# HGRN core of a two-block network on Trainium2: half products written in place, one buffer per level, and the decays computed beside the projection

## The chip, the cores and the metric

The kernel is written in Bass for one NeuronCore of a Trainium2 chip. The core has five engines with a queue of instructions each: TensorE (PE, with its weight loads shown apart as PEld), VectorE (DVE), ScalarE (ACT), GpSimd (POOL), and SyncE (SP), which here only issues DMAs. The engines meet at semaphores. The metric is the device time of one launch in microseconds (us).

## What is computed

Sequence length 512, model width 1024, batch 1. The change lies in the first layer (an "even" layer) of the first block: one projection of the input feeds an HGRN2 mixer with 4 heads of width 128 and a forgetting attention (FoX) with 8 heads of width 64; both are joined by an output projection. Three layers of other kinds follow and are not touched.

```python
proj = x @ ev_w_in[e]
qa, fa, ia, ga, qb, kb, vb, fb = split_cols(proj, [HALF] * 7 + [FOX_HEADS])
ya = hgrn2(qa, fa, ia, ga, lb_all[layer], ev_hgrn_norm_g[e])
yb = forgetting_attention(qb, kb, vb, fb, ev_fox_bf[e])
mix = jnp.concatenate([ya, yb], axis=-1) @ ev_w_out[e]

# hgrn2: the decays, and one step of its scan over chunks
log_f = jnp.log(lb + (1.0 - lb) * jax.nn.sigmoid(z))
k = (1.0 - lb) * jax.nn.sigmoid(-z)
b = jnp.cumsum(lt, axis=2)
o_inter = jnp.einsum('bhtk,bhkv->bhtv', qt * jnp.exp(b), state)
rel = b[:, :, :, None, :] - b[:, :, None, :, :]
decay = jnp.exp(jnp.where(causal, rel, -jnp.inf))
scores = jnp.einsum('bhtk,bhtsk,bhsk->bhts', qt, decay, kt)
o = o_inter + jnp.einsum('bhts,bhsv->bhtv', scores, vt)

# forgetting_attention: c is a running sum of log_sigmoid(f + b_f)
logits = logits + c[:, :, q0:q1, None] - c[:, :, None, :q1]
p = jax.nn.softmax(logits, axis=-1)
```

The decay between two positions differs by channel, so the kernel can't write the scores as one matmul. In chunks of 128 positions it splits the causal triangle into the diagonal (level 0) and 7 levels of off-diagonal blocks, whose side halves from one level to the next. In level i the decay of a pair is the product of a factor of the key (to the middle of its block) and one of the query (from there on), so each level is one set of matmuls of scaled keys with scaled queries, masked to the blocks of that level.

## The kernel before

`even_layer` (L1760) runs six stages one after the other, each closed by a barrier of all engines (`stage`, L64).

**Projection** (`linear_stage`, `linear_block`). 29 weight jobs of 512 KB are streamed. Per job ACT rounds the weights to a high part (L141), DVE subtracts to get the low part (L146), and PE does three matmuls for each of 8 tiles (L180 to L182). ACT writes the feature jobs 0 to 20 out of PSUM (L620), DVE the two groups of token jobs (L627). A `side` object can hang further work on each job j through `on_act`, `on_dve` and `on_pe`. The odd layer has one (`LruSide`), this layer has none.

**Constants** (`constants_stage`). DVE casts a few small masks.

**HGRN** (`hgrn_stage`, L1402). First a prologue: the lower bound `lb` from a softmax over three rows (L1522 to L1534), two sigmoids (L1448), the affine steps (L1537, L1540), one logarithm (L1468), and 16 scans of 128 columns for the running sums b (L1545). Then, per head, nine steps: for level i DVE subtracts the block's middle value from b (`take_diff`, L1557), ACT takes exp of the first half of each block with scale -1 (L1494) and of the second half with +1 (L1496), DVE multiplies all 512 columns with k (L1603) and POOL all 512 with q (L1636) into double buffers `ke` and `qe`. PE multiplies the two (L1679), DVE masks the result (`mask`, L1572), PE adds it into the output with v (`add_level`, L1652). `take_diff` runs one level ahead, and its two-deep buffers `diff` and `decay` are given back by L1603 and L1636. The ninth step is exp(b) for the state between chunks (L1477), followed by three state updates on DVE (L1616, L1619), POOL's `qd` (L1641) and three matmuls (L1708). Square (L1456), variance (L1661), logarithm and exp (L1461, L1464) and the gated write (`normed`, L1581, L1584) normalise the head before.

**FoX decay** (`fox_decay_stage`). One chain over DVE and ACT on 8 partitions, from L1721 to L1731, ends in `c_hi` and `c_lo`.

**Softmax attention** (`softmax_attention_stage`, L1284). 32 units, one for each block of 128 queries and head, with 128, 256, 384 and 512 keys for the blocks 0 to 3. Per unit PE writes q times k (L1786, contraction over 64 rows), adds c by two matmuls with a contraction over 8 rows each (L1789) and a bf16 mask (L1790), then transposes the exponentials of the unit before (L1322) and multiplies those of two units before with v (L1334). DVE finds the maximum (L1373), copies the transposed block (L1383), and scales the result (L1395); ACT does the exp (L1357).

**Output projection.** Another `linear_stage`. `keep_warm` (L346) is a helper that issues n matmuls of bf16 with 512 columns whose results nobody reads (L350); no stage from the first projection to the softmax calls it here.

## Time and profile before

| | |
|---|---|
| median of 3 runs | 3848.94 us (3837.36 to 3852.4) |
| profiled execution | 3850.37 us, of which its span in the trace is 3848.6 us |
| PE, DVE, ACT, POOL busy | 94%, 42%, 35%, 14% of the span |
| DMA | 76 GB/s over the span |

The busy shares are means over stages with different limits, so the rows further down are cut by stage. The table of stretches gives for each stretch its length, the busy time of each engine with the number of instructions, then `PEclk`, TensorE's granted clock as a share of 2.4 GHz (0.50 is the level of 1.2 GHz), the DMA share and GB/s. Timelines give start, duration, engine, line, operation, and in brackets the idle time before it and what ended it.

### The profile page before, as it was taken

What the parts mean: (1) busy time and instruction counts of PE and PEld (TensorE: products, weight loads), DVE (VectorE), ACT (ScalarE), POOL (GpSimd) and SP (SyncE); (2) the same over time, 40 slices, a digit from 0 to 9 for tenths busy, and PEclk for the clock granted to TensorE, in tenths of its full rate; (3) what the DMA queues carried; (4) which work ended last, traced back from release to release, by engine and by line L of the source; (5) the groups of instructions that cost most, each with busy time, mean ns of one, the idle gap of its engine ahead of it and who ended that gap; (6) DMA issues with size and microseconds to landing.
All of it is one profiled execution on the core that took longest, in us unless ns stands there. A gap on an engine that the chain in (4) does not pass through costs nothing. (4 is left out here: it accounts for less than half of the span.)

```text
span 3848.6 us, 42102 instructions
## 1 busy us (share of the span) xinstructions
PE 3598.5 (94%) x15648; PEld 2825.8 (73%) x15662; DVE 1619.7 (42%) x2091; ACT 1334.2 (35%) x1864; POOL 552.4 (14%) x446
## 2 busy tenths in 40 slices
PE   8878999998889999899998889999999999789998
PEld 7675668886666888688885468887788875578885
DVE  2284443335554333433345743335333235743335
ACT  3232232224553222433232543324333233533324
POOL 0030121101022110221000012202221000022202
PEclk9985899999999999999999899999999999899999
DMA  4200123322112332233220023322233220123322
GB/s 136 81 1 1 44 71 98 107 85 67 49 44 77 98 107 79 77 94 108 82 91 34 13 83 96 106 97 75 90 96 108 84 79 28 33 82 94 109 81 72
DMA packets 77745, 294.18 MB, mean 76 GB/s; under 512 B 8624, under 2 KB 11184, under 8 KB 77360
## 3 DMA queue, kind: packets, MB, share of 16 engines
q1 hardware_dynamic: 77616, 292.45, 23.9%
q8 instruction: 82, 1.34, 0.1%
q14 instruction: 47, 0.39, 0.0%
HBM read 290.32 MB, written 2.10 MB: 76 GB/s over the span
## 5 line engine op out<-in xcount | busy, mean ns | idle before, releaser
L146 DVE TENSOR_TENSOR w_low<-w_raw,w_high 128x1024 fp32r<-128x1024 f32 (+4 forms) x513 | 672.7, 1311 | 1578.5 <-ACT w_high L141 1578.5
L180 PE MATMUL bank<-x_high,w_high 128*128 128x512 f32 x2856 | 1130.4, 396 | 74.5 <-POOL x_low L224 22.0
L181 PE MATMUL bank<-x_low,w_high 128*128 128x512 f32 x2856 | 1120.4, 392 | 0.0
L182 PE MATMUL bank<-x_high,w_low 128*128 128x512 f32 x2856 | 1120.3, 392 | 0.0
L141 ACT CAST w_high<-w_raw 128x1024 fp32r<-128x1024 f32 (+4 forms) x513 | 555.0, 1082 | 872.8 <-PE bank L182 867.1
L180 PEld LDWEIGHTS bank<-x_high,w_high 128*128 128x128 f32 x2856 | 541.0, 189 | 206.4 <-issue 38.2
L182 PEld LDWEIGHTS bank<-x_high,w_low 128*128 128x128 f32 x2856 | 541.1, 189 | 113.3
L181 PEld LDWEIGHTS bank<-x_low,w_high 128*128 128x128 f32 x2856 | 541.9, 190 | 112.0 <-issue 2.1
L182 PE MATMUL bank<-hidden_high,w_low 128*128 128x512 f32 x1056 | 411.4, 390 | 0.0
L180 PE MATMUL bank<-hidden_high,w_high 128*128 128x512 f32 x1056 | 411.4, 390 | 0.0
L181 PE MATMUL bank<-hidden_low,w_high 128*128 128x512 f32 x1056 | 411.4, 390 | 0.0
L182 PEld LDWEIGHTS bank<-hidden_high,w_low 128*128 128x128 f32 x1056 | 198.3, 188 | 41.1
L180 PEld LDWEIGHTS bank<-hidden_high,w_high 128*128 128x128 f32 x1056 | 198.3, 188 | 41.1
L181 PEld LDWEIGHTS bank<-hidden_low,w_high 128*128 128x128 f32 x1056 | 198.3, 188 | 40.9
L901 POOL TENSOR_TENSOR hidden_and_gated<-hidden_and_gated,rstd 128x512 f32<-128x512 f32 x88 | 113.6, 1290 | 413.0 <-ACT hidden_and_gated L879 413.0
L905 POOL TENSOR_TENSOR hidden_low<-hidden_and_gated,hidden_high 128x512 f32 (+1 forms) x88 | 113.2, 1286 | 376.1 <-ACT hidden_high L883 376.1
L741 POOL TENSOR_TENSOR hidden_low<-hidden_and_gated,hidden_high 128x512 f32 (+1 forms) x44 | 56.9, 1294 | 434.9 <-ACT hidden_high L713 434.9
L883 ACT CAST hidden_high<-hidden_and_gated 128x512 f32 (+1 forms) x88 | 54.7, 622 | 175.5 <-DVE hidden_and_gated L939 175.5
L879 ACT ACTIVATE hidden_and_gated<-hidden_and_gated 128x512 f32<-128x512 f32 x88 | 55.6, 632 | 160.7 <-DVE hidden_and_gated L934 160.6
L713 ACT CAST hidden_high<-hidden_and_gated 128x512 f32 (+1 forms) x44 | 27.3, 621 | 212.3 <-DVE hidden_and_gated L767 212.3
L1357 ACT ACTIVATE probs<-bank,exp_bias 128x512 f32<-128x512 f32 (+3 forms) x64 | 38.8, 607 | 172.9 <-DVE exp_bias L1376 172.9
L1373 DVE TENSOR_REDUCE top<-bank 128x1 f32<-128x512 f32 (+3 forms) x64 | 37.9, 592 | 111.8 <-PE bank L1790 60.2
(481 smaller groups left out, 3799.9 us busy)
## 6 DMA issues: line engine op xcount, KB each, us to landing
w_raw<-in_stream SPq DMA_DIRECT2D x381, 512.0 KB, 3.5
w_raw<-in_stream SPq DMA_DIRECT2D x96, 704.0 KB, 4.0
w_raw<-in_stream SPq DMA_DIRECT2D x16, 384.0 KB, 3.1
dft_positions<-in_dft SPq DMA_DIRECT2D x2, 2048.0 KB, 7.4
w_raw<-in_stream SPq DMA_DIRECT2D x4, 576.0 KB, 3.7
h<-in_x SPq DMA_DIRECT2D x8, 256.0 KB, 6.0
w_raw<-in_stream SPq DMA_DIRECT2D x16, 128.0 KB, 2.1
out<-result SPq DMA_DIRECT2D x4, 512.0 KB, 2.6
```

What stands on the lines that cost most here:

```text
L141: self.nc.scalar.copy(self.hi[:, j % 2, 0:size], self.raw[:, s, 0:size]).then_inc(S.high_ready, 1)
L146: self.nc.vector.tensor_tensor(self.lo[:, j % 2, 0:size], self.raw[:, j % RAW_SLOTS, 0:size], self.hi[:, j % 2, 0:size].bitcast(F32), ALU. ...
L180: nc.tensor.matmul(out, lhs[0], rhs[0], start=start, stop=False)
L181: nc.tensor.matmul(out, lhs[0], rhs[1], start=False, stop=False)
L182: return nc.tensor.matmul(out, lhs[1], rhs[0], start=False, stop=stop)
L741: nc.gpsimd.tensor_tensor(hlo[:, at, :], hidden[:, u % 2:u % 2 + 1, :], hhi[:, at, :].bitcast(F32), ALU.subtract).then_inc(S.hid_low, 1)
L879: nc.scalar.activation(gated[:, u // 2, :], gated[:, u // 2, :], ACT.Silu).then_inc(S.gate_ready, 1)
L883: nc.scalar.copy(hhi[:, bass.ds(u // 2 + 2 * k, 1), :], hidden[:, u // 2, :]).then_inc(S.hid_high, 1)
L901: nc.gpsimd.tensor_tensor(gated[:, u % 2, :], gated[:, u % 2, :], C.rstd[:, :], ALU.mult).then_inc(S.gate_scaled, 1)
L905: nc.gpsimd.tensor_tensor(hlo[:, at, :], hidden[:, u % 2:u % 2 + 1, :], hhi[:, at, :].bitcast(F32), ALU.subtract).then_inc(S.hid_low, 1)
L1357: nc.scalar.activation(probs[:, n % 2, 0:keys(n)], C.bank[n % 2][:, 0:keys(n)], ACT.Exp, bias=bias[:, n:n + 1], scale=scale, accum_out=tot ...
L1373: nc.vector.tensor_reduce(top[:, n:n + 1], C.bank[n % 2][:, 0:keys(n)], AX.X, ALU.max).then_inc(S.top_ready, 1)
```

## The change

1. `DecaySide` is a side object of the projection. It takes over the whole HGRN prologue, the constants and the FoX decay: on ACT the first sigmoid (all four heads at once) after job 7, the second after job 12, the logarithm after job 14, FoX's steps after jobs 22, 23 and 25; on DVE the matching steps, four scans each after jobs 16 to 19. The level masks are fetched at the projection's start. The stages `constants_stage` and `fox_decay_stage` are gone.
2. After the last projection matmul PE issues 14 warm matmuls (`end_pe`); in the HGRN stage 8 stand ahead of the last variance and 24 behind it.
3. Level i has a buffer X[i] of its own. `take_diff` writes it, ACT's exps, DVE's product with k (first halves only, 256 columns) and POOL's with q (second halves only) are done in it in place, and PE reads it as both operands. `take_diff` runs two levels ahead, across heads. `normed(h)` moves to two heads later.
4. On PE a level's product now stands ahead of the `add_level` of two levels before, and the end of a head no longer stands in one piece: its last additions and its state product come behind the first levels of the next head.
5. In FoX `c_hi` and `c_lo` lie in one tile (partitions 0 to 7 and 64 to 71, zeros between), so one matmul over 72 rows takes the place of two over 8. It comes first, the mask second, q times k last.

```diff
+            if side:
+                side.end_pe(nc, C, pe, S)
...
-        diff, decay = C.ring[:, 0:2, :], C.ring[:, 2:4, :]
-        qe = sb("q_decayed", [P, 2, T])
-        ke = sb("k_decayed", [P, 2, T])
+        NL = LEVELS + 1
+        N = HALF_T * NL
+        more = sb("level_inputs", [P, NL - 4, T])
+        X = [C.ring[:, i, :] if i < 4 else more[:, i - 4, :] for i in range(NL)]
...
+                def decayed_k(m):
+                    h, i = m // NL, m % NL
+                    dve.wait_ge(S.decay_ready, 2 * (m + 1))
+                    x, kx = (halves(X[i], i)[0], halves(k[h], i)[0]) if i else (X[0], k[h])
+                    nc.vector.tensor_tensor(x, kx, x, ALU.mult).then_inc(S.k_ready, 1)
...
+                take_diff(0)
+                take_diff(1)
+                for m in range(N):
+                    h, i = m // NL, m % NL
+                    if m + 2 < N:
+                        take_diff(m + 2)
+                    decayed_k(m)
+                    if m >= 2:
+                        mask(m - 2)
+                    if i == 6:
+                        states(h)
+                    if h >= 2 and i == 1:
+                        normed(h - 2)
...
+                    if i:
+                        pool.wait_ge(S.decay_ready, 2 * (m + 1))
+                        x, qx = halves(X[i], i)[1], halves(q[h], i)[1]
+                        nc.gpsimd.tensor_tensor(x, qx, x, ALU.mult).then_inc(S.q_ready, 1)
...
+                add_level(N - 2)
+                add_level(N - 1)
+                keep_warm(nc, C, C.bank[0], 8)
                 variance(HALF_T - 1)
+                keep_warm(nc, C, C.bank[0], 24)
...
+    NEGATED, PLUS, LOGS, SCAN, FOX = 7, 12, 14, 16, 21
...
+        if j == self.NEGATED:
+            act.wait_ge(S.evacuated, 4 + 8)
+            nc.scalar.activation(self.kk[:, :, :], prj[:, 4:8, :], ACT.Sigmoid,
+                                 scale=-1.0).then_inc(S.negated, 1)
...
-                nc.tensor.matmul(bank[:, 0:keys], prj[r, 12 + t, qb * P:(qb + 1) * P],
-                                 prj[r, 16 + t, 0:keys], start=True, stop=False)
-                for part in (c_hi, c_lo):
-                    nc.tensor.matmul(bank[:, 0:keys], C.pick(h), part[:, 0:keys], start=False, stop=False)
+            nc.tensor.matmul(bank[:, 0:keys], C.pick_fox(h), c_parts[:, 0:keys], start=True, stop=False)
+            nc.tensor.matmul(bank[:, qb * P:keys], C.ident_bf, C.mask_after, start=False, stop=False)
+            return nc.tensor.matmul(bank[:, 0:keys], prj[r, 12 + t, qb * P:(qb + 1) * P],
+                                    prj[r, 16 + t, 0:keys], start=False, stop=True)
```

On ACT, in the projection, around jobs 7 and 8, the queue before reads (L141 is the high part of a weight job, L620 the write of a feature job):

```order
L620 ACTIVATE projections<-bank 128x512
L141 CAST w_high<-w_raw 128x1024
L620 ACT_TABLE_LOAD
L620 ACTIVATE projections<-bank 128x512
L141 CAST w_high<-w_raw 128x1024
```

and after the change (L622 is the same write, L1681 the first sigmoid):

```order
L622 ACTIVATE projections<-bank 128x512
L1681 ACT_TABLE_LOAD
L1681 ACTIVATE hgrn_k<-projections 128x2048
L141 CAST w_high<-w_raw 128x1024
L622 ACT_TABLE_LOAD
L622 ACTIVATE projections<-bank 128x512
```

A table load and a sigmoid of 2048 columns moved in between a job's write and the next job's high part; the same pattern stands after jobs 12 and 14.

On DVE, at the end of a head and the start of the next in the HGRN core, before (L1557 difference, L1603 product with k, L1572 mask, L1616 and L1619 state, L1596 level 0's product with k):

```order
L1603 TENSOR_TENSOR k_decayed<-hgrn_k,hidden_and_gated 128x512
L1572 TENSOR_TENSOR masked<-bank,level_masks 128x512 x2
L1616 COPY state<-bank 128x128
L1619 SCALAR_TENSOR_TENSOR state<-state,sq_sum_and_last,bank 128x128 x2
L1557 TENSOR_TENSOR hidden_and_gated<-projections 128x512 x2
L1596 TENSOR_TENSOR k_to_end<-hgrn_k,hidden_and_gated 128x512
L1572 TENSOR_TENSOR masked<-bank,consts 128x512
```

and after (L1498 difference, L1507 product with k, L1513 mask, L1527 and L1530 state):

```order
L1507 TENSOR_TENSOR level_inputs<-hgrn_k,level_inputs 128x128x2
L1513 TENSOR_TENSOR masked<-bank,level_masks 128x512
L1527 COPY state<-bank 128x128
L1530 SCALAR_TENSOR_TENSOR state<-state,sq_sum_and_last,bank 128x128 x2
L1498 TENSOR_TENSOR hidden_and_gated<-projections 128x512
L1507 TENSOR_TENSOR level_inputs<-hgrn_k,level_inputs 128x256
L1513 TENSOR_TENSOR masked<-bank,level_masks 128x512
L1498 TENSOR_TENSOR hidden_and_gated<-projections 128x512
L1507 TENSOR_TENSOR hidden_and_gated<-hgrn_k,hidden_and_gated 128x512
L1513 TENSOR_TENSOR masked<-bank,level_masks 128x512
```

The state updates now stand between levels 6 and 7 with the next head's difference already taken, and the products of levels 1 to 7 have 256 columns (as 128x128x2, 128x256).

On PE, where the HGRN stage ends, before (L1652 adds a level, L1708 the state product, L1661 the variance):

```order
L1652 MATMUL bank<-masked,hgrn_v 128x128 x8
L1708 MATMUL bank<-sq_sum_and_last,state 128x128 x3
L1661 MATMUL bank<-rstd,consts 128x512
L1435 UNCONDITIONAL_BRANCH
```

and after (L1584, L1594, L1601 are the same three, L350 the warm matmuls, then FoX's c, mask and q times k):

```order
L1584 MATMUL bank<-masked,hgrn_v 128x128 x12
L1594 MATMUL bank<-sq_sum_and_last,state 128x128 x3
L350 MATMUL bank<-consts_bf 128x512 x8
L1601 MATMUL bank<-rstd,consts 128x512
L350 MATMUL bank<-consts_bf 128x512 x24
L1440 UNCONDITIONAL_BRANCH
L1310 UNCONDITIONAL_BRANCH
L1798 MATMUL bank<-fox_c_parts,ident_fox 128x128
L1799 MATMUL bank<-consts_bf 128x128
L1800 MATMUL bank<-projections 128x128
```

32 warm matmuls stand around the last variance, and the softmax follows them with no stage between.

## Rows read from the trace of the kernel before

**Rows 1.** Table of stretches, by stage, columns as told above.

```profile
178.50:200.80 22.30, 2.09 (x9) 1.78 (x8) 13.88 (x43) 9.79 (x7) 0.00 (x0) 0.58 0.06 21
200.80:300.50 99.70, 80.32 (x570) 74.79 (x570) 88.94 (x114) 40.75 (x84) 42.25 (x32) 0.87 0.00 1
...
316.80:435.10 118.30, 116.80 (x416) 75.68 (x416) 45.52 (x160) 23.02 (x69) 0.00 (x0) 0.59 0.00 1
```

**Rows 2.** Timeline of ACT and DVE in the projection, one of the jobs.

```profile
43.79 0.60 ACT L620 ACTIVATE projections<-bank 128x512 f32<-128x512 f32 x1 [3.91 <-PE bank L182]
44.29 1.04 ACT L141 CAST w_high<-w_raw 128x1024 fp32r<-128x1024 f32 x1
...
45.36 1.23 DVE L146 TENSOR_TENSOR w_low<-w_raw,w_high 128x1024 fp32r<-128x1024 f32 x1 [4.21 <-ACT w_high L141]
```

**Rows 3.** Timeline, from the projection's end to the first level.

```profile
178.54 2.48 DVE L627 COPY fox_v<-bank 128x512 f32<-128x512 f32 x4 [3.08 <-PE bank L182]
181.93 0.36 DVE L1752 CAST consts_bf<-masks 128x384 bf16<-128x384 f32 x1 [0.90 <-PEq L64]
...
185.04 1.28 ACT L1448 ACT_TABLE_LOAD   x1
...
186.33 1.91 ACT L1448 ACTIVATE hgrn_k<-projections 128x2048 f32<-128x2048 f32 x1
```

**Rows 4.** Timeline of one level of the HGRN core (DVE, ACT, POOL).

```profile
262.58 0.68 DVE L1572 TENSOR_TENSOR masked<-bank,level_masks 128x512 f32<-128x512 f32 x1
...
263.19 1.52 DVE L1557 TENSOR_TENSOR hidden_and_gated<-projections 128x512 f32<-128x512 f32 x1
264.63 0.68 DVE L1603 TENSOR_TENSOR k_decayed<-hgrn_k,hidden_and_gated 128x512 f32<-128x512 f32 x1
...
265.60 1.27 POOL L1636 TENSOR_TENSOR q_decayed<-projections,hidden_and_gated 128x512 f32<-128x512 f32 x1 [1.44 <-ACT hidden_and_gated L1496]
265.83 1.58 DVE L1557 TENSOR_TENSOR hidden_and_gated<-projections 128x512 f32<-128x512 f32 x1
```

**Rows 5.** Stretches at the core's start and where its first head ends.

```profile
206.00:212.00 6.00, 5.34 (x25) 5.35 (x26) 5.29 (x6) 2.53 (x7) 2.77 (x2) 0.50 0.01 3
...
225.00:230.00 5.00, 2.88 (x23) 2.48 (x22) 4.86 (x8) 2.28 (x6) 1.47 (x2) 0.97 0.01 3
```

**Rows 6.** Timeline of DVE and PE at the end of the HGRN stage.

```profile
298.55 0.73 DVE L1619 SCALAR_TENSOR_TENSOR state<-state,sq_sum_and_last,bank 128x128 f32<-128x128 f32 x2
...
301.42 2.07 PE L1661 MATMUL bank<-rstd,consts 128*128 128x512 f32 x2 [0.88 <-ACT rstd L1456]
...
306.97 0.69 DVE L1584 TENSOR_TENSOR projections<-projections 128x512 f32<-128x512 f32 x1
```

**Rows 7.** Timeline: warm matmuls elsewhere in the kernel.

```profile
491.93 4.91 PE L350 MATMUL bank<-consts_bf 128*128 128x512 bf16 x22 [1.90 <-PEq L64]
```

**Rows 8.** Stretches of the softmax: blocks 0 to 3, its hot part, its tail.

```profile
316.80:333.30 16.50, 16.48 (x60) 12.09 (x60) 6.78 (x33) 4.52 (x16) 0.00 (x0) 0.50 0.01 1
333.30:360.00 26.70, 26.70 (x89) 17.81 (x88) 10.33 (x42) 5.37 (x19) 0.00 (x0) 0.50 0.00 0
360.00:397.00 37.00, 37.00 (x113) 22.99 (x112) 12.25 (x40) 5.87 (x18) 0.00 (x0) 0.50 0.00 1
397.00:411.50 14.50, 14.50 (x38) 7.59 (x38) 4.12 (x12) 1.55 (x4) 0.00 (x0) 0.50 0.01 1
415.00:427.10 12.10, 12.10 (x67) 7.57 (x66) 6.63 (x18) 3.12 (x8) 0.00 (x0) 1.00 0.00 0
427.10:435.10 8.00, 6.53 (x42) 4.71 (x41) 3.84 (x13) 1.80 (x5) 0.00 (x0) 1.00 0.00 0
```

**Rows 9.** Timeline of PE in one unit with 512 keys, at the full clock.

```profile
423.90 1.12 PE L1786 MATMUL bank<-projections 64*128 64x512 f32 x2
424.95 0.49 PE L1789 MATMUL bank<-fox_c_high,ident_parts 8*128 8x512 f32 x1
425.29 0.39 PE L1789 MATMUL bank<-fox_c_low,ident_parts 8*128 8x512 f32 x1
```

476 lines of the change are left out of this document (227 added, 249 removed).

## The prediction

> **What bounds the kernel now.** The busy shares of the page say little here (PE 94% of the span), since all that changes lies in the first 435 us; what follows is the same program. So I read the table of stretches first, cut by stage, then timelines of single steps. Four things are to be seen.
>
> The projection is PE's: a job takes 5.44 us, in which ACT works 1.6 us and DVE 1.23 us [rows 2]. Side work fits there nearly free.
>
> From 178.5 to 200.8 us PE is busy 2.1 us of 22.3 [rows 1]: two stage ends of about 0.9 us, the constants, and the prologue, a chain over ACT and DVE [rows 3]. The FoX decay is another such chain, from DVE's last write at 307.66 to 316.8 us [rows 6, 1].
>
> The HGRN core, 200.8 to 300.5, is DVE's: 88.9 of 99.7 us busy [rows 1]. A level takes 2.70 us from the end of one difference (263.19 + 1.52 = 264.71) to the end of the next (267.41) [rows 4]. That isn't three operations of 0.68. The difference of 1.58 us lies over POOL's product, which ends at 266.87, and it ends 0.54 us after it; alone it would take 0.68 like the mask. So the level is 0.89 (difference to POOL's start, through ACT's two exps) + 1.27 (POOL) + 0.54. At a head's end comes a hole in which PE is busy 2.88 of 5 us and its clock falls [rows 5].
>
> The softmax, 118.3 us, is PE's: busy nearly all of it, at 0.50, that is 1.2 GHz, for its first 95 us, and at 1.00 for its last 20 [rows 8]. Eight units with 384 keys take 37.0 us at the low level, 4.6 each; one with 512 keys takes only 3.20 at the high one (423.90 to 427.10, where the last begins) [rows 8, 9].
>
> **The change, part by part.** The sum is made against the profiled execution (span 3848.6, run 3850.4, which is 1.4 above the median of 3848.9; the saving is then taken off the median).
>
> Side work in the projection. After jobs 7, 12 and 14 ACT has, between a job's write and the next high part, one table load of 1.28 and one function over 2048 columns of 1.91 us [rows 3]. Chain per job: write 0.50 to the next start, 3.19 for the side work, high part 1.06, low part 1.23 = 5.98 against 5.44 [rows 2]. PE waits 0.54 us each, 1.6 in all. All other side work (DVE's products, 4 scans a job, small FoX steps with one table load each) fits DVE's 4.2 or ACT's 3.9 us of idle time per job. Bounds: 0 if slack in the two weight slots hides it, 6 if DVE's side steps add their wait each time. The level masks' DMA moves ahead of the weights' but lands long before its use.
>
> Here a row and the Trainium skill can be weighed: the load's row says 1.28 us [rows 3]. The page ScalarE: Activation LUTs gives two figures, about 2.7 us in its section Terms and 1283 ns in What ACT_TABLE_LOAD costs. By the first, each of the three steps would be 1.4 us longer and PE's wait 5.8 us instead of 1.6; the trace agrees with the second.
>
> Prologue. PE ends at 178.5 + 1.6 = 180.1; 14 warm matmuls at 4.91/22 = 0.22 us [rows 7] and their wait end at 183.3, 0.7 after DVE's last copy (182.6); one stage end of 0.95 [rows 3], so the first difference starts at 184.3 instead of 200.8. Gain 16.5.
>
> Core. POOL's product has 256 columns: between 0.64 (half of 1.27) and 1.27; DVE's 512 columns take 0.68 and 128-column updates 0.37 [rows 6], so a fixed part exists; I take 0.74. DVE's product with k drops from 0.6 to 0.34 effective. DVE's own step is then 0.6 + 0.34 + 0.6 = 1.55, and a difference is ready to start 0.94 after the last one, just after POOL has started (0.89). So the level is 0.89 + 0.74 + 0.54 = 2.17, with 1.55 (POOL never in the way) and 2.70 (half products cost as much as whole ones) as ends. Sum: start to the first k product 2.65 (difference, table load, exp); 32 levels x 2.17 = 69.4; states 4 x 1.05 = 4.2; POOL's whole `qd` in the way 4 x 0.6 = 2.4; two `normed`, each two operations like the one of 0.69 [rows 6], = 2.9; ACT's normalisation at two head changes x 2 = 4 (logarithm, exp and two table loads are some 4 us: 4.17 from the variance to DVE's end, less 1.4 of DVE, plus a load; with the wait for the variance that is longer than two levels of lead); PE's cold start 3 (before, it ran at 0.50 for its first 6 us too; 26 weight loads took 5.35 us there and 22 took 2.48 later [rows 5], so the 16 of a level 3.3 instead of 1.8); last masks, additions and state product 2.5. Total 91, against 99.7: gain 8.7, with 71 to 110 as ends. So the core gains least; the holes between heads go, but DVE remains late next, with PE close (1.8 us of weight loads per level at the full clock).
>
> A rule speaks against this part: the page GPSIMD Engine Reference of the Trainium skill, section 7, says of kernels written for POOL's own cores that reads of SBUF with a step over 8 bytes cost half as much again per element. If the second halves' runs of 2 to 8 columns fell under it, 12 of 28 products would be 0.37 us longer and the core 4 us. No run here shows POOL on such runs yet.
>
> Tail. 8 warm matmuls 1.7, variance 1.0 at the full clock (2.07 at half [rows 6]), 24 warm matmuls 5.3, which end after the normalisation's ACT and DVE steps (4.2 us behind the variance). 8.2 against 7.1 (300.54 to 307.66): loss 1.1.
>
> FoX decay. 9.1 us become one stage end of 0.9: gain 8.2.
>
> Softmax. This decides. Fewer matmuls: one of two c matmuls goes, 0.34 us at the full clock with 512 keys [rows 9]. At half it lies between 0.34 and 0.68; I take 0.57, and 0.3, 0.36 and 0.45 with 128, 256 and 384 keys. If the clock stays as it was, that is 8 x (0.3 + 0.36 + 0.45) + 3 x 0.57 + 5 x 0.33 = 12. But PE now comes in at the full clock: warm matmuls until 0.9 us before the first score. Then a unit is, for blocks 3 to 0: 3.20 - 0.33 = 2.9 (PE); about 2.2 (PE); 1.7 and 1.45 (DVE: maximum, copy, scale and two small steps, no longer under PE). 7 x 2.9 + 8 x (2.2 + 1.7 + 1.45) + tail 7.7 = 71 against 118.3: gain 47.5.
>
> Sum: 16.5 + 8.7 - 1.1 + 8.2 + 47.5 = 79.8. Profiled 3850.4 - 79.8 = 3770.6; off the median 3769.
>
> **The rivals.** (A) *The clock stays up through the softmax*: 3769. For it: where the clock fell in this trace, PE had been busy about half of 5 us or less [rows 5]; once up in block 3 it stayed, and with 128 keys PE would have work for over half of each 1.45 us. Against: 95 us of nearly full busy time didn't bring it up before [rows 8], so contractions over 8 or 64 rows and short matmuls may count for little, and block 0 may lose it.
>
> (B) *It falls in block 0 and returns in block 1 or 2*, as the denser units allow: blocks 0 and 1 near the old pace less c (14 + 24), the rest half and half: 91 instead of 71, so 3789.
>
> (C) *It falls and returns only in block 3*, as before: softmax 106, so 3849 - 45 = 3804.
>
> (D) *The half products don't shorten a level* (POOL's time is not by columns, or its lock hits the k product too): 32 x 0.53 = 17 more on A, 3786.
>
> (E) *Slower than before*: PE's clock stays at 1.2 GHz from the start of the core to the output projection. Place: levels. PE then needs 3.3 us a level where DVE needs 2.17, which is 36, and 10 for variance, transposes and state at half; warm matmuls +10; softmax without its hot end 116, +45: 3769 + 101 = 3870. It decides once cold time costs over 80 us. Against it: the same level stream brought the clock up within 7 us after every fall [rows 5].
>
> (F) *The change doesn't do what it says*: side work isn't hidden because DVE's and ACT's side steps wait on each other and hold the next weight job. 29 jobs; each microsecond of wait per job is one lost. It would take over 2.7 us on every job to lose all; I see it on 3 jobs. A bad case is +10: 3779, inside A's range.
>
> **How the numbers follow.** A 0.55, B 0.12, C 0.17, D (with the clock up) 0.11, E 0.02, other 0.03. I forecast A: 3769. A alone spans 3753 (level near 1.8, no wait in the projection, softmax 67) to 3782. The range must reach over B, D and C to leave out no more than 2 in 10: 3753 to 3807. A measurement of this kernel tells 0.5% (19 us) from no change; faster than 3829.7 are A to D and F: 0.95; within 0.5% only C with a bad core: 0.03; slower, E: 0.02.
>
> **What would show each step right or wrong.** Projection: PE's end at 180 us, three waits for w_low of about 0.5 us, table loads of 1.28. Prologue: first difference near 184 us. Core: half products of 0.34 to 0.42 on DVE and 0.64 to 0.8 on POOL, a step near 2.2 us, `PEclk` 1.00 from some 10 us after the start without dips at heads, length near 91. Softmax: `PEclk` 1.00 from its first unit and a length near 71; 106 with 0.50 in blocks 0 to 2 would be C. Everything after the softmax: the same 3413 us. I would be most wrong if the clock in block 0 doesn't hold, or if the level isn't set by the pair of DVE and POOL.

## The result, and the profile after

The changed kernel took **3782.59 us** (median of 4 runs, 3781.46 to 3785.99) against 3850.67 us for the kernel before (4 runs, 3837.36 to 3857.32). The ratio is 0.9829, with a 95% interval of 0.9802 to 0.9856: 68 us faster, where 80 had been forecast. The profiled execution took 3781.46 us, with a span of 3779.6.

First the table of stretches of the changed kernel, which answers to [rows 1 and 8]. The columns are as there: the stretch, its length, busy time of PE, PE's weight loads, DVE, ACT and POOL with their instructions, the granted clock, DMA share and GB/s. The lines are the prologue, the core, the softmax, and the part of the softmax at the low clock.

```profile
181.60:185.60 4.00, 2.97 (x14) 1.18 (x13) 2.49 (x4) 0.00 (x0) 0.00 (x0) 1.00 0.00 0
185.60:265.30 79.70, 72.55 (x578) 68.26 (x580) 70.14 (x114) 40.29 (x84) 34.74 (x32) 0.96 0.01 1
274.40:360.50 86.10, 84.46 (x384) 58.99 (x384) 46.09 (x160) 21.74 (x68) 0.00 (x0) 0.74 0.00 1
277.60:321.60 44.00, 44.00 (x151) 31.23 (x151) 20.66 (x83) 9.75 (x35) 0.00 (x0) 0.50 0.00 1
360.50:3779.60 3419.10, 3245.75 (x13956) 2544.64 (x13970) 1420.44 (x1727) 1205.18 (x1634) 502.98 (x406) 0.97 0.25 80
```

Set against the trace of before this is where the 69.0 us of the span went. The stages follow each other without a gap, so the differences add up. The table compares one execution of each kernel; the four runs of the kernel before lie 20 us apart, those of the changed kernel 4.5.

| stretch | before | after | gained | forecast |
|---|---|---|---|---|
| start to the last evacuation's start | 178.5 | 181.6 | -3.1 | -1.6 |
| to the first difference (prologue) | 22.3 | 4.0 | 18.3 | 18.1 |
| core | 99.7 | 79.7 | 20.0 | 8.7 |
| core's end to the first score | 16.3 | 9.1 | 7.2 | 7.1 |
| softmax | 118.3 | 86.2 | 32.1 | 47.5 |
| the rest, the same program | 3413.5 | 3419.1 | -5.6 | 0 |

(The forecast's 16.5 for the prologue already holds the 1.6 that the projection loses, and its last tail terms, -1.1 and 8.2, stand together here.)

**The core.** The timeline of DVE through two levels, which answers to [rows 4] (start, length, engine, line, operation):

```profile
205.35 0.68 DVE L1513 TENSOR_TENSOR masked<-bank,level_masks 128x512 f32<-128x512 f32 x1
205.95 0.68 DVE L1498 TENSOR_TENSOR hidden_and_gated<-projections 128x512 f32<-128x512 f32 x1
206.55 0.41 DVE L1507 TENSOR_TENSOR hidden_and_gated<-hgrn_k,hidden_and_gated 128x256 f32<-128x256 f32 x1
206.88 0.68 DVE L1513 TENSOR_TENSOR masked<-bank,level_masks 128x512 f32<-128x512 f32 x1
207.49 0.68 DVE L1498 TENSOR_TENSOR level_inputs<-projections 128x512 f32<-128x512 f32 x1
208.09 0.95 DVE L1507 TENSOR_TENSOR hidden_and_gated<-hgrn_k,hidden_and_gated 128x256 f32<-128x256 f32 x1
208.96 0.68 DVE L1513 TENSOR_TENSOR masked<-bank,consts 128x512 f32<-128x512 f32 x1
```

and POOL's in the same stretch:

```profile
205.13 0.89 POOL L1569 TENSOR_TENSOR hidden_and_gated<-projections,hidden_and_gated 128x256 f32<-128x256 f32 x1 [0.25 <-ACT hidden_and_gated L1467]
207.46 1.29 POOL L1569 TENSOR_TENSOR hidden_and_gated<-projections,hidden_and_gated 128x256 f32<-128x256 f32 x1 [1.45 <-ACT hidden_and_gated L1467]
209.00 0.73 POOL L1569 TENSOR_TENSOR level_inputs<-projections,level_inputs 128x256 f32<-128x256 f32 x1 [0.24 <-ACT level_inputs L1467]
```

Before, the difference was what POOL held up, 1.58 us instead of 0.68. Now it takes 0.68 here. Over the whole core a difference takes 0.73 us in the mean, where it took 1.13. The two engines still get in each other's way, but on short work: where POOL's product starts together with a difference, the product takes 1.29 instead of 0.73, and DVE's product behind it 0.95 instead of 0.41 (0.75 in the mean of all 28). From mask to mask a level took 1.53 (205.35 to 206.88) and 2.08 us (206.88 to 208.96). What is left is one wait at two of the three changes of heads, 3.00 and 2.50 us; the longer one:

```profile
220.13 0.68 DVE L1498 TENSOR_TENSOR hidden_and_gated<-projections 128x512 f32<-128x512 f32 x1
223.81 0.69 DVE L1507 TENSOR_TENSOR hidden_and_gated<-hgrn_k,hidden_and_gated 128x512 f32<-128x512 f32 x1 [3.00 <-ACT hidden_and_gated L1463]
```

ACT is late there because it stands before its logarithm until PE's variance comes (the first line ends with 4.43 us of idle time), loads the table of the exponential, and only then turns to the next head:

```profile
220.63 0.69 ACT L1453 ACTIVATE rstd<-bank,eps 128x512 f32<-128x512 f32 x1 [4.43 <-PE bank L1601]
221.34 1.28 ACT L1456 ACT_TABLE_LOAD   x1
222.63 0.63 ACT L1456 ACTIVATE rstd<-rstd 128x512 f32<-128x512 f32 x1
223.17 0.61 ACT L1463 ACTIVATE hidden_and_gated<-hidden_and_gated 128x512 f32<-128x512 f32 x1
```

**From the core to the softmax.** PE's timeline, which answers to [rows 6]. The last five lines are the start of the fourth unit of block 0; up to 277.35 the same three score matmuls took 0.30, 0.23 and 0.49 us.

```profile
265.35 1.67 PE L350 MATMUL bank<-consts_bf 128*128 128x512 bf16 x7
266.86 1.02 PE L1601 MATMUL bank<-rstd,consts 128*128 128x512 f32 x2
267.72 5.34 PE L350 MATMUL bank<-consts_bf 128*128 128x512 bf16 x24
274.37 0.30 PE L1798 MATMUL bank<-fox_c_parts,ident_fox 72*128 72x128 f32 x1 [1.30 <-PEq L64]
274.51 0.23 PE L1799 MATMUL bank<-consts_bf 128*128 128x128 bf16 x1
274.67 0.49 PE L1800 MATMUL bank<-projections 64*128 64x128 f32 x2
...
277.35 0.46 PE L1798 MATMUL bank<-fox_c_parts,ident_fox 72*128 72x128 f32 x1
277.61 0.33 PE L1799 MATMUL bank<-consts_bf 128*128 128x128 bf16 x1
277.87 0.79 PE L1800 MATMUL bank<-projections 64*128 64x128 f32 x2
278.60 0.47 PE L1324 MATMUL bank<-consts,probs 128*128 128x128 f32 x1
278.86 0.63 PE L1336 MATMUL bank<-fox_v,probs_t 128*128 128x128 f32 x2
```

PE comes in at 2.4 GHz, as forecast, with a pause of 1.30 us, and 3 us later it is at 1.2 GHz. It stays there for 44 us, into block 2. That is rival B of the prediction, not its forecast A.

**The rest.** Same program, 5.6 us longer. Read in stretches of 2 us, its time at the low clock grew from 188.7 to 211.7 us; in the stick-breaking stage, for one, the kernel before had three spells with 17.1 us together (1014 to 1040 us in), and the changed kernel has nine with 37.6 us (939 to 1039 us in).

### The profile page after: what moved, and what is told of

It is laid out like the page before. It is cut to its first block and busy times, and to the rows that moved or that the text cites. A ratio compares the mean times of both kernels' runs of the same rounds, so it can differ in the third digit from the quotient of the medians.

```text
span 3779.6 us, 41993 instructions
## 1 busy us (share of the span) xinstructions
PE 3575.7 (95%) x15660; PEld 2809.0 (74%) x15676; DVE 1601.5 (42%) x2095; ACT 1334.5 (35%) x1864; POOL 544.8 (14%) x446
## 5 line engine op out<-in xcount | busy, mean ns | idle before, releaser
L141 ACT CAST w_high<-w_raw 128x1024 fp32r<-128x1024 f32 (+4 forms) x513 | 555.0, 1082 | 867.9 <-PE bank L182 862.7
L769 DVE TENSOR_TENSOR hidden_and_gated<-bank,hidden_and_gated 128x512 f32<-128x512 f32 x44 | 30.4, 692 | 120.6 <-PE bank L182 120.6
```

The lines of the kernel that those rows point to most:

```text
L141: self.nc.scalar.copy(self.hi[:, j % 2, 0:size], self.raw[:, s, 0:size]).then_inc(S.high_ready, 1)
L769: nc.vector.tensor_tensor(hidden[:, u // 2, :], C.bank[u][:, :], gated[:, u // 2, :], ALU.mult).then_inc(S.hid_ready, 1)
```

## The experiments

All were single profiled runs beside the kernel before, but for the last two, which were timed five and six times. The table gives the lengths of the stages, read as above; "cold" is the time at 1.2 GHz from the core's end to the softmax's end, read in stretches of 2 us, and the stretch in which it lies.

| kernel | run | prologue | core | to first score | softmax | cold | rest |
|---|---|---|---|---|---|---|---|
| changed kernel | 3781.5 | 4.0 | 79.7 | 9.1 | 86.2 | 44 (276-322) | 3419.1 |
| a1 no end warm | 3781.8 | 4.0 | 79.7 | 7.4 | 87.7 | 51 (270-324) | 3419.2 |
| a2 two c matmuls | 3810.1 | 4.0 | 80.5 | 9.1 | 116.5 | 92 (278-372) | 3415.6 |
| a3 warm beside units | 3757.0 | 4.0 | 79.7 | 9.1 | 70.8 | 3 (276-282) | 3410.2 |
| a4 128 rows | 3778.4 | 4.0 | 79.8 | 9.1 | 86.1 | 44 (278-324) | 3415.5 |
| c1 before, half products | 3845.6 | 24.6 | 86.3 | 15.4 | 124.0 | 119 (296-416) | 3413.8 |
| c2 one level ahead | 3783.8 | 4.0 | 78.0 | 9.1 | 92.4 | 58 (276-336) | 3415.6 |
| c3 decays apart | 3800.7 | 28.8 | 79.4 | 8.6 | 86.2 | 44 (298-344) | 3416.4 |
| c4 q.k first | 3781.8 | 4.0 | 79.7 | 9.1 | 89.5 | 48 (276-326) | 3415.8 |
| d1 split and root later | 3758.4 | 4.0 | 74.6 | 9.1 | 75.3 | 21 (266-290) | 3415.6 |
| d2 four warm units | 3756.7 | 4.0 | 80.7 | 9.1 | 67.6 | 0 | 3410.4 |
| d3 all three | 3763.0 | 4.0 | 74.7 | 7.4 | 81.2 | 31 (262-294) | 3413.6 |
| e1 end warm kept | 3761.9 | 4.0 | 74.7 | 9.1 | 77.7 | 24 (268-292) | 3415.3 |

### The clock in the softmax

The theory after the result: the clock is lost at the change of stages or in block 0's thin matmuls, and where it returns depends on how many matmuls a unit has. The rivals: the 32 warm matmuls at the core's end cost more than they bring; the number of rows over which the c matmul runs counts.

**a1**: without the warm matmuls at the core's end.

```
-                keep_warm(nc, C, C.bank[0], 8)
                 variance(HALF_T - 1)
-                keep_warm(nc, C, C.bank[0], 24)
```

> The changed kernel without the 8 and 24 warm matmuls at the end of the HGRN stage. In the changed kernel the softmax began at the full clock and lost it 3.3 us later. If the warm matmuls buy only those 3 us, the softmax is 1 to 4 us longer (87 to 90 instead of 86.2) and the HGRN tail 3 to 4 us shorter (9.1 to about 6), so the first 360 us end within 2 us of the changed kernel. If they also bring forward the return of the clock in block 2, the softmax is over 8 us longer.

Measured: the way to the first score is 1.7 us shorter, not 3 to 4, the softmax 1.5 us longer, and the run as long as the changed kernel's. The clock fell 6 us earlier, ahead of the softmax, and came back at nearly the same place. In this kernel the 32 matmuls are neither gain nor loss: the clock is low for most of block 0 with them and without.

**a2**: the decay's parts by two matmuls over 8 rows, as in the kernel before.

```
-            nc.tensor.matmul(bank[:, 0:keys], C.pick_fox(h), c_parts[:, 0:keys], start=True, stop=False)
...
+            for part in (c_parts[0:8, :], C.c_lo[:, :]):
+                nc.tensor.matmul(bank[:, 0:keys], C.ident_parts[0:8, h:h + 1].to_broadcast([8, P]), part[:, 0:keys],
+                                 start=False, stop=False)
```

> The changed kernel with FoX's scores as before: q times k first, then c_hi and c_lo as two matmuls over 8 rows each, then the mask. Theory 1 (what counts for the clock's return is how much of the array's height and time is filled; two thin matmuls dilute it): the clock returns only in block 3, as before (some 14 us into it), and the softmax takes 100 to 108 us instead of 86.2. Theory 2 (the return depends on what came before the softmax, not on the c matmul): it returns in block 2 and the softmax takes 86.2 + 12 for the additional matmuls at most 98.

Measured: 30 us longer in the softmax. That is far more than the matmuls themselves, some 12 us by the prediction's sum. The clock now stays low until block 3, 92 us instead of 44. All three kernels with two c matmuls (this one, the kernel before, and c1 below) got it back only there.

**a3**: two warm matmuls (bf16, 384 columns) beside each unit of block 0, one beside each of block 1, written into the bank of the turned probabilities ahead of them.

```
+                        for w in range(warm[units[m][0]]):
+                            nc.tensor.matmul(C.bank[2 + m % 2][:, 0:3 * P], C.ident_bf, C.con_bf[:, 0:3, :],
+                                             start=True, stop=True)
                         pe.wait_ge(S.exp_done, m + 1)
...
+        softmax_attention_stage(nc, C, HEADS, HD, scores, vb, prj, 4, True, 1.0, warm=(2, 1, 0, 0))
```

> The changed kernel with warm matmuls of 384 columns inside the softmax, in TensorE's wait for the exp: two in each unit of block 0, one in each of block 1. If the thin work of block 0 is what loses the clock, it stays at 1.00 through the softmax, which then takes 70 to 77 us instead of 86.2 and the program is 10 to 16 us shorter than the changed kernel. If the clock falls anyway (the gap at the stage's start is what loses it), the softmax is longer than 86 by the warm matmuls at the low clock, 88 to 95.

Measured, stretches of 2 us over the start of this kernel's softmax, then its whole softmax:

```profile
276.00:278.00 2.00, 2.00 (x13) 1.52 (x11) 1.23 (x6) 0.97 (x6) 0.00 (x0) 0.80 0.00 0
278.00:280.00 2.00, 2.00 (x9) 1.40 (x9) 0.91 (x5) 0.31 (x3) 0.00 (x0) 0.50 0.00 0
280.00:282.00 2.00, 2.00 (x14) 1.66 (x13) 1.31 (x7) 0.43 (x3) 0.00 (x0) 0.84 0.00 0
282.00:284.00 2.00, 2.00 (x15) 1.51 (x14) 1.65 (x9) 0.67 (x4) 0.00 (x0) 1.00 0.00 0
...
274.30:345.20 70.90, 69.40 (x408) 48.80 (x408) 45.94 (x160) 21.78 (x68) 0.00 (x0) 0.98 0.00 1
```

The clock falls at the same moment as in the changed kernel and is back after 3.4 us of low clock in all. Neither of the two cases expected is what happened: it neither stayed up nor stayed down. The softmax takes 70.8 us, close to the prediction's 71 for case A, a state that the changed kernel doesn't reach; but these 70.8 hold the low spell and 24 warm matmuls.

**a4**: the c matmul over 128 rows instead of 72, the further ones zero.

```
-        c_parts = ctx.enter_context(sbuf(nc, "fox_c_parts", [72, T], F32R))
+        c_parts = ctx.enter_context(sbuf(nc, "fox_c_parts", [P, T], F32R))
...
-        C.pick_fox = lambda h: C.ident_fox[:, h:h + 1].to_broadcast([72, P])
+        C.pick_fox = lambda h: C.ident_fox[:, h:h + 1].to_broadcast([P, P])
```

> The changed kernel with the c tile padded to 128 rows of which the added ones are zero, so the c matmul runs over 128 rows instead of 72, with the same columns. Theory 1a (rows of the array, even with zeros in them, count for the clock): the clock returns earlier, in block 1, and the softmax takes 70 to 80 us. Theory 1b (only columns streamed per time count): it returns at the same place within 4 us and the softmax stays at 85 to 88.

Measured: no difference (86.1 against 86.2 us, 44 us at the low clock in both). Rows of zeros changed neither the softmax's time nor the clock.

**c4**: one c matmul, but q times k ahead of it, as in a2. It asks whether a2's late return came from the order.

```
-            nc.tensor.matmul(bank[:, 0:keys], C.pick_fox(h), c_parts[:, 0:keys], start=True, stop=False)
-            nc.tensor.matmul(bank[:, qb * P:keys], C.ident_bf, C.mask_after, start=False, stop=False)
-            return nc.tensor.matmul(bank[:, 0:keys], prj[r, 12 + t, qb * P:(qb + 1) * P],
...
+            nc.tensor.matmul(bank[:, 0:keys], prj[r, 12 + t, qb * P:(qb + 1) * P],
+                             prj[r, 16 + t, 0:keys], start=True, stop=False)
+            nc.tensor.matmul(bank[:, 0:keys], C.pick_fox(h), c_parts[:, 0:keys], start=False, stop=False)
+            return nc.tensor.matmul(bank[:, qb * P:keys], C.ident_bf, C.mask_after, start=False, stop=True)
```

> The changed kernel with the three matmuls of a score in another order: q times k first, then the one matmul over the 72 rows of parts of the decay, the mask last. Two causes are to be told apart for the clock's earlier return in the softmax (44 us cold in the changed kernel, 92 us with two matmuls for the decay's parts and q times k first). By the number of matmuls: the clock returns in block 2 at about 320 us, and the softmax takes 84 to 90 us. By the order: it returns only in block 3, and the softmax takes 105 to 117 us.

Measured: the clock returned in block 2 and the softmax took 89.5 us. So the order isn't it; the second matmul over 8 rows is what goes with the late return. How firm that is, the end of this section says: five kernels with one and the same softmax program lie between 21 and 58 us at the low clock.

### The core and the prologue

**c1**: the kernel before, with the half products alone. The cut shows k's; q's on POOL is made the same way with the other halves, and both operands are cleared once ahead of the loop.

```
-                            nc.vector.tensor_tensor(ke[:, i % 2, :], k[h], decay[:, m % 2, :],
+                            nc.vector.tensor_tensor(half_of(ke[:, i % 2, :], i, 0), half_of(k[h], i, 0),
+                                                    half_of(decay[:, m % 2, :], i, 0),
...
```

> The kernel before with one part of the change alone: k's and q's products of a level over the half of the columns that the next level's matmul needs (256 of 512), their two operands each cleared once ahead of the loop. The differences still run one level ahead through the small buffers, the extra two steps per head and the decays stay where they were. Theory 1 (the products were the core's bound: per level the difference 0.89 us, the k product 0.73, the mask 0.54 on VectorE, and a q product of half the length on GpSimd that no longer bars VectorE): the core falls from 99.7 us to about 84 to 88, that is three quarters or more of the 20 us that the core gained. Theory 2 (looking two levels ahead and the merged heads gave most of it): the core stays at 92 us or more. Nothing outside the core should move by over 1 us except where TensorE's clock falls and returns in the softmax; the total is about 3825 to 3840 us.

Measured: core 86.3 us, inside theory 1's 84 to 88, but that is 13.4 of the 20.0 us, two thirds and not three quarters. The total, 3845.6, lay above the 3825 to 3840 expected, with 124.0 us in the softmax and 24.6 in the prologue. The stretch and DVE's groups in a part of it:

```profile
204.20:290.50 86.30, 73.09 (x570) 69.11 (x570) 67.73 (x114) 40.39 (x84) 29.84 (x32) 0.92 0.01 1
...
L1565 DVE TENSOR_TENSOR hidden_and_gated<-projections 128x512 f32<-128x512 f32 x23 | 18.2, 799 | 0.0
L1580 DVE TENSOR_TENSOR masked<-bank,level_masks 128x512 f32<-128x512 f32 x21 | 14.5, 688 | 9.4 <-PE bank L1689 9.0
```

DVE is busy 67.7 us here, less than in the changed kernel's core (70.1), but it is idle for 18.6, and 9.4 of that, in this part of 60 us alone, stand before masks, for PE's product of the level just handed over. In the changed kernel a mask comes two levels behind, and that idle time is 1.7 us in the whole core. The masks' distance is thus the likely source of much of the other third. It was not run apart from the merged heads, nor from the 14 warm matmuls after the projection: the clock granted to this core is 0.92, against 0.96 in the changed kernel and 0.87 before [rows 1], and a slower PE hands the masks their product later.

**c2**: the differences one level ahead instead of two.

```
                 take_diff(0)
-                take_diff(1)
...
-                    if m + 2 < N:
-                        take_diff(m + 2)
+                    if m + 1 < N:
+                        take_diff(m + 1)
```

> The changed kernel with the differences taken one level ahead instead of two; all else as changed. Theory 1 (two levels ahead keep VectorE fed while the exponential of the level before is under way): the core grows from 79.7 us to 86 or more, since each level then holds the chain difference, exponential, product (about 0.69 + 0.9 + 0.5 us and the handing over) with little beside it. Theory 2 (the half products did it alone): the core stays within 2 us of 79.7. Projection, prologue (4.0 us) and the end of the core to the first score (9.1 us) stay.

Measured:

```profile
187.00:265.00 78.00, 71.06 (x579) 67.20 (x580) 68.34 (x114) 40.61 (x85) 33.66 (x32) 0.98 0.00 1
```

The core takes 78.0 us, 1.7 less than with two levels. Theory 1 falls: the second level ahead brings nothing here. The likely reason is that with masks two levels behind DVE has a mask of 0.68 us and more to do while ACT's exponentials run. That one level is better than two isn't shown, since the clock was higher too, 0.98 against 0.96 (in a2 and d2, whose core's program is the changed kernel's, 3.4 us more at the low clock went with a core 0.8 and 1.0 us longer).

**c3**: the decays in a stage of their own behind the projection.

```
-                         source=Input("plain", C.h, DT, arrivals=C.x_in),
-                         side=DecaySide(nc, ctx, work, prj, kk, masks, c_parts))
+                         source=Input("plain", C.h, DT, arrivals=C.x_in))
+            side = DecaySide(nc, ctx, work, prj, kk, masks, c_parts)
+            with stage(nc, "evacuated" + side.SEMS) as S, nc.Block() as block:
...
```

> The changed kernel with the decays' steps in a stage of their own behind the projection instead of beside it. What is expected if the gain ahead of the core came from hiding these steps: PE is done with the projection at 178.5 us as in the kernel before (3.1 us earlier than now), and the time from the last evacuation to the first difference grows from 4.0 us to about 25 (22.3 in the kernel before, and a stage more); the total is then about 18 to 24 us over the changed kernel's. If instead a better order of the same steps gave part of it, the stretch is clearly under 20 us.

Measured: 28.8 us from the last evacuation to the first difference, against 4.0, and 19.2 us in the run. PE is busy 4.6 of them:

```profile
179.50:208.20 28.70, 4.60 (x14) 1.61 (x14) 18.10 (x52) 14.86 (x13) 0.00 (x0) 0.69 0.05 16
```

The last evacuation started 2.2 us earlier (179.46 against 181.64), not 3.1; 0.6 us of that lie ahead of the projection's first write (22.64 against 22.00), so the side work costs the projection some 2.8 us. The gain ahead of the core is the hiding, all of it.

### A version that beats both

**d1**: two edits. The side work's long activations in halves, one a job; the root of a head's variance after the exponentials of the next head's first two levels. With them `normed` comes one level later, the second sigmoid one job earlier and the scans one job later.

```
-            nc.scalar.activation(self.kk[:, :, :], prj[:, 4:8, :], ACT.Sigmoid,
+            nc.scalar.activation(self.kk[:, 0:2, :], prj[:, 4:6, :], ACT.Sigmoid,
                                  scale=-1.0).then_inc(S.negated, 1)
...
+        if j == self.NEGATED + 1:
+            nc.scalar.activation(self.kk[:, 2:4, :], prj[:, 6:8, :], ACT.Sigmoid,
+                                 scale=-1.0).then_inc(S.negated, 1)
...
-                    if h and i == 7:
-                        rstd(h - 1)
+                    if h >= 2 and i == 1:
+                        rstd(h - 2)
+                rstd(HALF_T - 2)
```

> The changed kernel with two edits at places that don't meet. First, the two sigmoids and the logarithm of the side tasks, 2048 columns each (1.92 us on ScalarE), are cut into pieces of 1024 columns, one piece a job. Second, ScalarE takes the reciprocal root of a head's variance after the exponentials of the next head's first two levels instead of before them. If the projection's 3.1 us are what the weight's halves wait for behind the long pieces, they fall to under 1.5 us, and PE's projection ends at 180.1 us or earlier; if they come from the table loads instead (1.28 us each, now more of them), they stay at 3 us or grow. If VectorE's two waits of 3.00 and 2.50 us at head changes are those for ScalarE's root, the core falls from 79.7 to about 74 to 76; if they are the wait for something else that comes late at the same place, it stays over 78. The softmax may move by several us with the point at which the clock returns; that is no part of either theory.

The first operation of PE in a job, by groups over the projection (busy us, mean ns | idle before it and what ended it). The changed kernel's line first:

```profile
L180 PEld LDWEIGHTS bank<-x_high,w_high 128*128 128x128 f32 x109 | 20.5, 188 | 7.4 <-DVE w_low L146 3.3
```

and that of d1:

```profile
L180 PEld LDWEIGHTS bank<-x_high,w_high 128*128 128x128 f32 x110 | 20.6, 188 | 5.0 <-DVE w_low L146 0.7
```

The wait for the low halves falls from 3.3 to 0.7 us although there are more table loads, and the last evacuation starts at 177.93. Part of that is the clock: from 150 to 178 us it was 1.00 here and 0.94 in the changed kernel and in d3 and e1, where the same projection with the same 0.7 us of waits ended at 180.32 and 179.28. In the core, waits for ACT before the first product of a head were 6.3 us in the changed kernel (5.5 of them at two head changes); here:

```profile
L1508 DVE TENSOR_TENSOR hidden_and_gated<-hgrn_k,hidden_and_gated 128x512 f32<-128x512 f32 x4 | 4.4, 1088 | 0.8 <-ACT hidden_and_gated L1463 0.8
```

The core takes 74.6 us, 5.1 less. Both causes are confirmed, the long pieces and the root. The softmax took 75.3 us, with no edit there: the clock fell at 266 and returned at 290, sooner than in any other kernel without warm matmuls beside the units. The changed kernel, a1, c2 and c3 have this softmax program too, and were at the low clock for 44, 51, 58 and 44 us.

**d2**: the changed kernel with warm matmuls beside the first four units only.

```
+                        for w in range(warm[units[m][0]] if m < 4 else 0):
```

> The changed kernel with two bf16 warm matmuls of 384 columns beside each of the first four units of the softmax only, that is in half of block 0. With them in all 16 units of blocks 0 and 1 the clock was back after 6 us and the softmax took 70.8 us; without them it came back in block 2 and the softmax took 86.2 us. Theory 1 (the clock is lost at the change of stages, and once it is back the stage itself keeps it): the softmax takes 70 to 74 us, with under 6 us cold. Theory 2 (block 0's own short fp32 matmuls don't hold the clock): it falls again within blocks 0 and 1, with 25 us or more cold, and the softmax takes 80 us or more.

```profile
276.80:344.40 67.60, 65.90 (x392) 46.13 (x392) 45.69 (x160) 21.82 (x68) 0.00 (x0) 1.00 0.00 1
```

The clock never fell. Behind the fourth unit nothing was added, and 2.4 GHz held, which speaks for theory 1; but see e1. And up to the fourth unit a3 is the same program as d2, yet its clock fell 3 us into the softmax. So what PE does in block 0 doesn't decide alone whether the clock falls there.

**d3**: d1's edits, a3's warm matmuls, and a1's removal of those at the core's end (the edits as above).

> The changed kernel with what the runs have shown so far put together: warm matmuls beside the units of blocks 0 and 1 of the softmax (two and one a unit), the side tasks' long activations cut in two, the root of the variance taken after the next head's first two levels, and without the 32 warm matmuls at the core's end. If the gains add: projection 1.5 to 2 us less, core 4 to 5, end of the core to the first score 1.7, softmax 15 less than the changed kernel's 3779.6 us in the profiled span, and up to 9 us less in the rest, as with the warm matmuls alone; about 3745 to 3757 us, against 3755.3 for the warm matmuls alone. If the gains don't add (the rest's cold spells move against them), it stays between 3757 and 3780 us.

Measured: 3761.66 us median (5 runs, 3755.16 to 3762.99), ratio 0.9781 (0.9759 to 0.9803). Core and end gave what they had given singly, and the projection's waits were 0.7 us again. The softmax didn't: without matmuls at the core's end the clock was low from 262 to 294 us, and took until then to return in spite of the warm matmuls.

**e1**: d1's edits with d2's warm matmuls, and those at the core's end kept.

> The kernel before this one (the long activations cut in two, the root of the variance later) with two differences: the 32 warm matmuls at the core's end are back, and those beside the softmax's units are only at its first four units, two a unit. Theory 1 (the clock is lost at the change of stages from the core to the softmax; matmuls at the core's end and beside the first units carry it over, and behind that the stage keeps it): no more than 7 us cold between 258 us and the softmax's end, softmax 67 to 72 us, projection, prologue, core and end as in the runs that had them (177.9, 4.0, 74.6, 9.1 us), and 3740 to 3750 us in all. Theory 2 (where the clock falls and returns depends on the moment the softmax is reached, and these cases are luck): 20 us or more cold there, as with the cut activations alone, and 3754 to 3764 us.

Measured: 3759.94 us median (6 runs, 3754.6 to 3771.51), ratio 0.9779 (0.9757 to 0.9801), clear of the changed kernel's 0.9802 to 0.9856 by a hair; its runs lie 17 us apart, the changed kernel's 4.5. The softmax of the profiled run:

```profile
267.00:344.70 77.70, 76.21 (x392) 53.52 (x392) 45.81 (x160) 21.81 (x68) 0.00 (x0) 0.85 0.00 1
```

24 us cold, where d2 with the same softmax program had none. Theory 1 said at most 7; its rival, that the moment counts, said 20 or more. So what decides whether the clock falls, and how soon it is back, is **open**. It isn't plain noise between executions either: the changed kernel's four runs all had a mean granted clock of 0.963 to 0.965. The seven kernels of the table with one c matmul and no warm ones beside the units had 21 to 58 us cold (six of them 44 and more), the four with warm matmuls beside units 0 to 31. They help, but don't settle it.

## Why the prediction was right, and where its steps were wrong

The time, 3782.6, lay in the range of 3753 to 3807, and 68 us were gained where 80 were forecast. Two steps missed by over 10 us, in opposite directions: the softmax gained 15.4 us less than forecast and the core 11.3 more. That they nearly cancel is luck, and the range held because it had been drawn over the rivals B, C and D.

**Softmax: the choice of case failed.** The step was that PE, once it comes in at the full clock, keeps it through all units, case A, with a chance of 0.55. PE did come in at 2.4 GHz and lost it 3 us into block 0 (the timeline above). What happened is B, given 0.12 and priced at 91 us for the softmax; it took 86.2. The sizes under it held within a few us: A's 71 stands against 67.6 in d2, the one kernel that had no low clock there (with 8 warm matmuls in it), and a unit of 512 keys takes 2.84 us, forecast 2.9:

```profile
350.00 0.48 PE L1798 MATMUL bank<-fox_c_parts,ident_fox 72*128 72x512 f32 x1
...
352.84 0.48 PE L1798 MATMUL bank<-fox_c_parts,ident_fox 72*128 72x512 f32 x1
```

The evidence that I set against A and then weighed too low was [rows 8]: 95 us of a nearly fully busy PE at 1.2 GHz. The same thin stream that doesn't bring the clock up can't be trusted to hold it, though in d2 it held it through 28 units without help. B's and C's border was one matmul a unit: with two (a2) the return moved to block 3, and the run, 3810.1, to where C had been priced, 3804.

**Core: the level was mis-sized.** Mechanism and place were right (half products shorten POOL's hold on DVE; 0.73 for POOL alone, forecast 0.74; 0.41 for DVE), the level was not. I forecast 2.17 us, that each difference would still be held until POOL is done. The differences take 0.73 in the mean; POOL's product and the k product are what wait, 0.57 and 0.54 us, in every other level or so. A level is then 1.53 and 2.08 us by turns, some 0.37 less than forecast, and 32 of them are the 11 us. By DVE's busy time: levels, states, `qd` and normalisation were priced at 69.4 + 4.2 + 2.4 + 2.9 = 78.9 us, and DVE was busy 70.1. The other terms, start, head changes, cold start and end, were priced at 12.2 and DVE was idle 9.6. Of the head changes (2 us each), two cost 3.00 and 2.50, for the reason given, and d1 took them away. That looking two levels ahead matters, which the change suggests and my head-change term leaned on ("longer than two levels of lead"), was not borne out by c2.

**Projection: right place, half the size.** Three waits for w_low, as forecast, but 3.3 us in all instead of 1.6. The chain per job was right: after job 7's write, which starts at 60.08, the low half is done at 66.10, 6.02 us later, forecast 5.98. What failed is what it was set against. The sum took 5.98 less the 5.44 us of a job, 0.54. But PE's first matmul of job 9, which needs that low half, was due 5.24 us after that write's start (the last of job 8's starts at 65.09, and they follow each other at 0.23), so PE was held from 65.32 to 66.16, 0.84 us, and its first matmul behind the wait took 0.1 us longer. From write to write the two jobs after job 7 took 11.85 us instead of 10.88: 0.97 lost, three times, is 2.9 of the 3.1 us.

```profile
60.70 1.28 ACT L1681 ACT_TABLE_LOAD   x1
61.99 1.92 ACT L1681 ACTIVATE hgrn_k<-projections 128x2048 f32<-128x2048 f32 x1
63.81 1.03 ACT L141 CAST w_high<-w_raw 128x1024 fp32r<-128x1024 f32 x1
64.86 1.28 ACT L622 ACT_TABLE_LOAD   x1
64.87 1.23 DVE L146 TENSOR_TENSOR w_low<-w_raw,w_high 128x1024 fp32r<-128x1024 f32 x1 [7.44 <-ACT w_high L141]
66.15 0.19 PEld L180 LDWEIGHTS bank<-x_high,w_high 128*128 128x128 f32 x1 [1.09 <-DVE w_low L146]
```

The table load ahead of the next write, the last ACT line, isn't the cause. The kernel before has one at the same place, and d1, which has two such loads (at 64.35 and 69.79), waits 0.7 us in all:

```profile
61.66 1.28 ACT L620 ACT_TABLE_LOAD   x1
```

After jobs 12 and 14 there is none, other than the section on the change says (the write behind job 12's high part starts without one), and PE's weight loads wait 1.09 and 1.10 us there too:

```profile
91.98 1.03 ACT L141 CAST w_high<-w_raw 128x1024 fp32r<-128x1024 f32 x1
93.69 0.60 ACT L622 ACTIVATE projections<-bank 128x512 f32<-128x512 f32 x1 [0.68 <-PE bank L182]
```

Here a figure that was weighed before can be settled: all loads in this trace took 1.28 us. The Trainium skill, page ScalarE: Activation LUTs, has about 2.7 us in its section Terms; its section What ACT_TABLE_LOAD costs gives 1283 ns for the load and about 1380 ns of a drain beside it. The trace agrees with the load's figure and shows no drain: the write ends at 60.68, the load runs from 60.70 to 61.98, and the sigmoid starts at 61.99.

**POOL's reads with a step.** Half products of level 4 (runs of 8 columns) took 0.72 us, like level 3's, and those of levels 6 and 7, runs of 2 and of 1, took 0.84 in c1:

```profile
257.89 0.85 POOL L1645 TENSOR_TENSOR q_decayed<-projections,hidden_and_gated 128x256 f32<-128x256 f32 x1 [0.30 <-ACT hidden_and_gated L1502]
260.18 0.84 POOL L1645 TENSOR_TENSOR q_decayed<-projections,hidden_and_gated 128x256 f32<-128x256 f32 x1 [1.44 <-ACT hidden_and_gated L1502]
```

Half as much again, which the page GPSIMD Engine Reference of the Trainium skill, section 7, gives for kernels on POOL's own cores that read with a step over 8 bytes, would be 1.08 us. No run shows it for these instructions.

**Prologue and tail** were right to 0.2 us: the first difference 4.0 us after the last evacuation's start, 9.1 us from the core's end to the first score, and c3 shows that hiding is the whole cause. PE waited for no other step of the side work and not for the level masks' DMA. (In the tail two small misses cancel: 7.8 us up to the last warm matmul's end, where 8.2 was forecast and the three terms give 8.0, and a pause of 1.30 instead of 0.9.)

**The rest** was taken as the same program and the same time. It was 5.6 us longer, and between 3410.2 and 3419.2 us in the kernels above. Its clock falls and returns at places that move with what came before; that is a term of 9 us that I had left out.

## What to carry to other kernels

Half products pay because they shorten what one engine holds against another, so count a level by which instruction waits, and read it again after the change: here the waiting moved from a 0.68 us difference that blocked everything to products that have slack. Before building a second level of lookahead, try one level with the consumer moved further behind; here it was enough. Don't price a stage at the full clock because PE enters it at the full clock: look whether the same instructions have ever raised or held it in the trace, and give "it falls and returns later" the larger chance where they have not.

## What the runs showed of the hardware

- A PE that is busy all the time can stay at 1.2 GHz: 44.00 of 44.0 us busy at 0.50 in the changed kernel's softmax, 92 us in a2. One matmul over 8 rows more in each unit goes with 48 us more of it (a2 against the changed kernel). Zero rows beside the real ones (a4) changed nothing.
- Bf16 matmuls of 384 columns beside the same thin fp32 stream went with a return within 6 us (a3) or no fall at all (d2), but not always: 24 us cold in e1, 31 in d3. The same softmax program without them had 21 to 58 us in five kernels (changed kernel, a1, c2, c3, d1) that differ only in what stands ahead of it.
- From d2 (0 cold, 67.6 us) to the changed kernel (44 cold, 86.2) each microsecond at the low clock costs this softmax 0.42 us, not 0.5, presumably because part of its time is DVE's, which no run measured by itself.
- DVE and POOL hold each other up in both directions. A 256-column product takes 0.41 us on DVE alone and 0.95 behind POOL's, and 0.73 on POOL alone and 1.29 beside DVE's difference.
- The logarithm and the exponential of the variance's root load a table each, 1.28 us, every time (four times in the changed kernel's HGRN stage, as at 214.92 and 221.34), and each of the two sigmoids and the logarithm beside the projection loads one. A way back isn't always paid: the write after the first sigmoid has a load, as in the kernel before, those after the second sigmoid and the logarithm have none.
